# The difference of the two attention maps formed whole by VectorE

## What is computed

```
s = jnp.einsum('bqhmd,bkhmd->bhmqk', qi, k_all).astype(jnp.float32) * scale
p = jax.nn.softmax(s, axis=-1)
a = p[:, :, 0] - lam * p[:, :, 1]
return jnp.einsum('bhqk,bkhe->bqhe', a.astype(v_all.dtype), v_all)
```

## Time and profile before

| what | value |
| --- | --- |
| median of three runs | 2513.55 us |
| profiled execution, first to last instruction | 2509.4 us |
| TensorE busy over the whole span | 2317.3 us, 92% |
| VectorE busy | 1323.7 us, 53% |
| ScalarE busy | 849.3 us, 34% |
| GpSimd busy | 875.1 us, 35% |
| mean granted TensorE clock | 0.974 |

### The profile page before, as it was taken

One profiled execution on the slowest core, in us unless ns is written; L12 is line 12 of the kernel. 1 busy time (PEld: TensorE's weight loads), 2 busy tenths in 40 slices (PEclk: granted clock), 3 DMA queues, 4 the chain that ended last, 5 costly groups with the idle time before them and its releaser, 6 DMA issues. The chain is left out here.

```text
span 2509.4 us, 30851 instructions
## 1 busy us (share of the span) xinstructions
PE 2317.3 (92%) x10898; PEld 1846.8 (74%) x10898; DVE 1323.7 (53%) x1373; ACT 849.3 (34%) x1244; POOL 875.1 (35%) x600
## 2 busy tenths in 40 slices
PE   4799999999968999999999999968888888899998
PEld 2445888888746788887787788857777777788787
DVE  5754339999992200016556540079999995800101
ACT  5745511111101212222222211157777774222221
POOL 0004823333311222221221222136656653844443
PEclk9999999999989999999999999989999997999999
DMA  8977621111111122221221232332221105153433
GB/s 290 337 247 219 193 66 46 50 46 46 46 42 51 55 72 71 67 72 54 72 75 53 72 97 72 87 89 57 59 59 48 48 1 206 67 176 127 160 129 108
DMA packets 227184, 246.46 MB, mean 98 GB/s; under 512 B 11277, under 2 KB 163853, under 8 KB 225583
## 3 DMA queue, kind: packets, MB, share of 16 engines
q1 hardware_dynamic: 225680, 235.11, 29.8%
q0 software_dynamic: 1440, 10.49, 1.1%
HBM read 214.09 MB, written 31.47 MB: 98 GB/s over the span
## 5 line engine op out<-in xcount | busy, mean ns | idle before, releaser
L448 POOL TENSOR_TENSOR w_lo<-w_raw,w_hi 128x512 fp32r<-128x512 f32 x288 | 402.7, 1409 | 1067.3 <-ACT w_hi L700 1066.9
L570 PE MATMUL psum<-h_hi,w_hi 128*128 128x512 f32 x1792 | 561.6, 395 | 6.5 <-POOL w_lo L448 4.9
L570 PE MATMUL psum<-h_hi,w_lo 128*128 128x512 f32 x1792 | 552.8, 390 | 0.0
L570 PE MATMUL psum<-h_lo,w_hi 128*128 128x512 f32 x1792 | 552.6, 390 | 0.0
L700 ACT ACTIVATE w_hi<-w_raw 128x512 fp32r<-128x512 f32 x288 | 180.8, 631 | 1036.9 <-PE psum L570 729.6
L570 PEld LDWEIGHTS psum<-h_hi,w_hi 128*128 128x128 f32 x1792 | 337.3, 188 | 85.3 <-issue 16.5
L570 PEld LDWEIGHTS psum<-h_lo,w_hi 128*128 128x128 f32 x1792 | 337.1, 188 | 70.6
L570 PEld LDWEIGHTS psum<-h_hi,w_lo 128*128 128x128 f32 x1792 | 336.9, 188 | 70.3
L999 DVE SCALAR_TENSOR_TENSOR conv<-y_pad,tap_w,conv 128x1024 f32<-128x1024 f32 x240 | 365.2, 1522 | 9.4
L1675 POOL TENSOR_TENSOR wo_lo<-wo_raw,wo_hi 128x512 fp32r<-128x512 f32 x128 | 175.8, 1380 | 188.4 <-ACT wo_hi L1758 188.4
L84 PE MATMUL psum<-wo_hi,m_hi 128*128 128x512 f32 x512 | 202.0, 395 | 10.7 <-DVE m_lo L1791 6.5
(11 more groups left out here) (174 smaller groups left out, 3182.8 us busy)
## 6 DMA issues: line engine op xcount, KB each, us to landing
w_raw<-in_w_in_dram SPq DMA_DIRECT2D x288, 256.0 KB, 3.0
ada_w<-in_w_ada_dram SPq DMA_DIRECT2D x32, 1024.0 KB, 6.8
wo_raw<-in_w_out_dram SPq DMA_DIRECT2D x128, 256.0 KB, 3.0
proj<-stage SPq DMA_DIRECT2D x40, 512.0 KB, 3.1
gate_w<-in_w_ada_dram SPq DMA_DIRECT2D x16, 1024.0 KB, 5.0
x_tok<-in_x_dram POOLq DMA_DIRECT2D x8, 1024.0 KB, 7.2
k_raw<-proj SPq DMA_DIRECT2D x16, 512.0 KB, 5.7
q_raw<-proj SPq DMA_DIRECT2D x16, 512.0 KB, 6.2
```

Of the source, the lines that this page charges most:

```text
L448: pool.tensor_tensor(w_lo[:, c], w_raw[:, c], w_hi[:, c].bitcast(F32), ALU.subtract).then_inc(w_lo_ready[c], 1)
L570: mm = pe.matmul(bank(2 * s_ + hf), w[:, c, j, :], x[:, jj, hf * BANK:(hf + 1) * BANK], start=(jj == 0 and w is w_hi and x is h_hi), stop= ...
```

## The change

VectorE's scalar_tensor_tensor now covers all 1280 columns. `difference_rest`, its semaphore `rest_ready` and the three places that waited for it (TensorE before round 1 of `turn_diff`, ScalarE before `exp`, GpSimd before its own second instruction and before `low_q`) are gone. GpSimd keeps `low_k` and `low_q` alone, each of which starts as soon as ScalarE's rounding has signalled; between the two kinds stands a wait for GpSimd's own earlier work.

```diff
-    SHARE = 6 * P
...
-                if rd == 1:
-                    pe.wait_ge(rest_ready, 2 * s_ + 2)
...
-                    act.wait_ge(rest_ready, 2 * s_ - 2)
...
-            def difference_rest(st, s_, first=False):
-
-                pool.wait_ge(factor_ready, s_ + 1)
-                if not first:
-                    pool.wait_ge(turned6, use6(s_ - 2, 1) + 1)
-                b = st % 2
-                rest = diff[:, b, SHARE:]
-                pool.tensor_tensor(rest, prob[:, b, 1, SHARE:], map1_factor[:, b:b + 1].to_broadcast([P, KEYS - SHARE]),
-                                   ALU.mult).then_inc(rest_ready, 1)
-                pool.wait_ge(rest_ready, 2 * s_ + 1)
-                pool.tensor_tensor(rest, rest, prob[:, b, 0, SHARE:], ALU.add).then_inc(rest_ready, 1)
-
-            def head(h, b, first=False, last=False):
-                for st in range(TT):
-                    s_ = TT * h + st
-                    if not last or st + 1 < TT:
-                        difference_rest((st + 1) % TT, s_ + 1, first and st == 0)
-                    if not last and st in (1, 2):
-                        low_k(h + 1, 1 - b, st - 1)
-                    if not last and st in (3, 4):
-
-
-                        pool.wait_ge(rest_ready, 2 * s_ + 4)
-                        low_q(h + 1, 1 - b, st - 3)
-                        pool.wait_ge(q_split, 2 * (h + 1) + st - 2)
-
...
+            def head(h, b):
+                for m in range(2):
+                    low_k(h + 1, 1 - b, m)
+                pool.wait_ge(k_split, 2 * (h + 2))
+                for m in range(2):
+                    low_q(h + 1, 1 - b, m)
+                    pool.wait_ge(q_split, 2 * (h + 1) + m + 1)
...
-                nc.vector.scalar_tensor_tensor(out=diff[:, st % 2, 0:SHARE], in0=prob[:, st % 2, 1, 0:SHARE],
-                                               scalar=map1_factor[:, st % 2:st % 2 + 1], in1=prob[:, st % 2, 0, 0:SHARE],
+                nc.vector.scalar_tensor_tensor(out=diff[:, st % 2, :], in0=prob[:, st % 2, 1, :],
+                                               scalar=map1_factor[:, st % 2:st % 2 + 1], in1=prob[:, st % 2, 0, :],
                                                op0=ALU.mult, op1=ALU.add).then_inc(diff_ready, 1)
```

More of the change, by code:

```diff
@@ L1140, in attention @@
     factor_ready = sem("factor_ready")
-    rest_ready = sem("rest_ready")
     diff_ready = sem("diff_ready")
@@ L1377, in low_q @@
                                    ).then_inc(q_split, 1)
-            def difference_rest(st, s_, first=False):
-                pool.wait_ge(factor_ready, s_ + 1)
-                if not first:
-                    pool.wait_ge(turned6, use6(s_ - 2, 1) + 1)
-                b = st % 2
-                rest = diff[:, b, SHARE:]
-                pool.tensor_tensor(rest, prob[:, b, 1, SHARE:], map1_factor[:, b:b + 1].to_broadcast([P, KEYS - SHARE]),
-                                   ALU.mult).then_inc(rest_ready, 1)
-                pool.wait_ge(rest_ready, 2 * s_ + 1)
-                pool.tensor_tensor(rest, rest, prob[:, b, 0, SHARE:], ALU.add).then_inc(rest_ready, 1)
-            def head(h, b, first=False, last=False):
-                for st in range(TT):
-                    s_ = TT * h + st
-                    if not last or st + 1 < TT:
-                        difference_rest((st + 1) % TT, s_ + 1, first and st == 0)
-                    if not last and st in (1, 2):
-                        low_k(h + 1, 1 - b, st - 1)
-                    if not last and st in (3, 4):
-                        pool.wait_ge(rest_ready, 2 * s_ + 4)
-                        low_q(h + 1, 1 - b, st - 3)
-                        pool.wait_ge(q_split, 2 * (h + 1) + st - 2)
-            difference_rest(0, 0, first=True)
-            head(0, 0, first=True)
+            def head(h, b):
[5 more added lines that the diff above has]
+                    pool.wait_ge(q_split, 2 * (h + 1) + m + 1)
+            head(0, 0)
             with pool.Fori(0, HEADS // 2 - 1) as i:
@@ L1410, in _ @@
                 head(2 * i + 2, 0)
-            head(HEADS - 1, 1, last=True)
         @block.vector
```

## The result

The kernel with the whole difference on VectorE takes 2531.46 us in the median (2527.77 to 2534.07, 4 runs), beside 2514.08 for the kernel before in the same session: slower by 17.4 us, ratio 1.0071 [1.0057, 1.0086]. The forecast was 2536.5 in a range of 2519 to 2544, with slower at 0.83. So sign and range hold, the size is 5 us too large. The time is also the very number of rival 1, by coincidence: the trace has the forecast's mechanism, `factor` held, at smaller prices.

What follows compares the result with a forecast made beforehand. VectorE, busy 51.4 of 54 us a head, was taken to set the pace. Per head 1.15 + 1.80 + 0.15 = 3.1 us; seven heads 21.7, last head 1.2: 2513.55 + 22.9 = 2536.5 us, range 2519 to 2544.

Steps and rivals of the forecast that it cites:

- rival 1: Small `factor` is not held by GpSimd, only the difference: 2.4 us a head, 2531.5 us; chance 0.20.
- step 1: Loop step of a head, counted from 0, where the first `k_lo` was to hold `factor`: 1.15 us in all.
- step 3: Loop step of a head, counted from 0, where both `q_st` run and the second holds the difference: 1.80 us.
- `k_lo`, 1.15 forecast: First `k_lo` holds `factor` 1.1 us; with the difference at 1.56 instead of 1.51, 1.15 us a head.
- `q_st`, 1.80 forecast: First `q_st` holds `factor` some 0.7 us, hidden; the second holds the difference, delaying VectorE's next instruction 1.80 us a head.
- The widening: VectorE's difference at 1280 columns takes 1.56 us alone: 0.15 us a head elsewhere, 1.2 us in the last head.
- visible gaps: VectorE's idle times in a head: 0.51 us awaiting an exponential, about 0.5 us awaiting `dT_hi` in each value-turning step.
- Rival 2: GpSimd's splits hold nothing that matters, only the widening costs, some 2.5 to 3.5 us: 2516.5 us; chance 0.11.
- Rival 3: TensorE's wait on GpSimd's product is real, so 9.6 us go: 2507 us; chance 0.06.
- Rival 4: More is held: second `k_lo` catches a `factor`, or 1280 columns take 1.68 us: 2542 to 2550 us; chance 0.11.
- three value steps: Steps of a head that turn values; VectorE's idle wait for `dT_hi` was to hide the 1.56 us difference: cost nothing.

Runs made afterwards that it cites:

- both-placed kernel: Changed kernel with both `k_lo` and both `q_st` on GpSimd waiting for VectorE's differences: 2511.46 us, 0.9988 of the kernel before; longer second series 2512.74 us, 0.9993.
- Q's split placed: Changed kernel with only the two `q_st` waiting for VectorE's differences, `k_lo` as changed: 2519.55 us, 1.0020 of the kernel before.
- 15.3 us less VectorE work: Kernel before (768 columns on VectorE), GpSimd's share started after VectorE's difference, `factor` as one-input `tensor_scalar`: 2515.58 us, 1.0008.
- My three misses: Kernel before, GpSimd's share after VectorE's difference, `tensor_scalar` `factor`; VectorE at 768 columns, 896, or a share by step: 2515.58, 2517.02, 2515.22 us.
- three kernels with such different work on VectorE: Kernel before, and two edits of it with GpSimd's share after VectorE's difference and `tensor_scalar` `factor`: 768 columns (2515.58 us), share by step (2515.22 us).
- the freed VectorE: Kernel before with 768 columns on VectorE, GpSimd's share started after VectorE's difference, `factor` by `tensor_scalar`: 2515.58 us, 1.0008.
- one-input `factor`: Changed kernel with `factor` by `tensor_scalar`, one tile and two per-row scalars, GpSimd's queue as changed: 2532.77 us, 1.0076 of the kernel before.
- Q's split placed and the one-input `factor`: Changed kernel with both `q_st` waiting for VectorE's differences and `factor` by `tensor_scalar`, `k_lo` as changed: 2514.77 us, 1.0007 of the kernel before.

## Why the prediction was right, and where its sizes were off

**The mechanism.** All of its steps are in the trace: least duration of the difference 1.54 (1.56 forecast), one `map_factor` a head in step 1 at 1.20, in the first head 1.48 (about 1.3), one at 0.89 in step 3 (about 0.9), one difference at 2.65 (near 2.5), projections and output as before. The both-placed kernel shows that the two splits are the entire loss: put them behind the difference and the stretch falls by 18.75 us, more than the 17.31 it had gained. The open point, whether a 128 x 1 instruction is held, is settled: yes, and the one-input form beside the same `k_lo` is not. That agrees with the rule cited from the Trainium skill (SBUF — State Buffer, "SBUF: two separate sides"), which names two SBUF inputs and makes no exception for size.

**`k_lo`, 1.15 forecast, 0.98 measured.** `k_lo` starts 1.76 us ahead of `factor` where I placed 1.62: its rounding ends 0.11 earlier in the head, and it starts 0.08 after it, not 0.15. That is 0.14 less hold. The widening that I added behind it isn't seen.

**`q_st`, 1.80 forecast, 1.5 measured.** The hold itself is worth 1.72: step 3 grows by 1.65 with it, by -0.07 with Q's split placed. The pair takes 4.81 us, not 4.92, the gap between them being under a tenth. The other 0.16 is a gain that I had not seen: the wait of `p_inv` goes from 0.51 to 0.32, and step 3's `map_factor` comes 0.15 earlier. The both-placed kernel has the same -0.15 in each steady head, so it belongs to the change without the holds. I did not isolate it.

**The widening, 0.15 a head and 1.2 in the last forecast, 0 and about 0.6 measured.** This is the mis-sized term whose reason matters. I took each 0.05 us on VectorE outside the visible gaps for 0.05 us of the head. In the last head six differences grow by 0.12 each, and only every second one moves the next step, by 0.13; with the 0.28 of the very last (1.54 for the 1.26 of the earlier trace rows) that makes 0.6. In the steady heads nothing is left at all: where nothing is held, in the both-placed kernel, a steady head is 0.24 us shorter than before instead of 0.15 longer.

**The sum.** Forecast 7 x 3.1 + 1.2 = 22.9 us. Measured: the first head 2.65, the second 2.0, five at 2.46, the last 0.3, together 17.3, and 17.4 in the medians. Set against the both-placed kernel a steady head splits up cleanly: the two holds cost 0.97 and 1.72 us, 2.7 together, where 1.1 and 1.80 were forecast, and the rest of the change gives 0.24 back, where it was forecast to cost 0.2. So most of the 0.64 us a head lies in the rest of the change, not in the holds; seven heads multiply it.

**What bounds the kernel, half right.** "A microsecond put on VectorE outside these gaps is a microsecond of the attention" holds for time put where something waits: the 2.7 us of holds in a head came through whole. The opposite, time taken off, does not hold: 15.3 us less VectorE work gave nothing. The 10 us more of the both-placed kernel cost nothing either, but nearly all of that had been forecast to vanish in the gaps. My three misses rest on that reading. That the steady heads of three kernels with such different work on VectorE agree to 0.03 us says that something else sets their length. My reading is another loop, in which VectorE, TensorE and ScalarE wait for each other in turn (transposes, `dT_hi`, `dT_lo`, the product, the next scores, the maximum and the exponential that frees their bank); the waits of VectorE on `dT_hi`, on scores and on the exponential in the trace above are its joints. TensorE alone isn't the pace: with the freed VectorE it still waits 38 of 306 us in the steady heads. That loop is argued from the waits, and which of its links would have to become shorter was not tested and stays open.

**The rivals.** Rival 1 falls by the 1.20 and 0.89 us of `factor`. Rival 2 (no hold, 2516.5) is what the both-placed kernel builds, and even there the widening that it kept costs nothing. Rival 3, TensorE's wait on GpSimd: the purest test is the both-placed kernel, where GpSimd forms no part of the difference and nothing is held. Its waits of TensorE in the steady heads:

```profile
PE psum L1199 <- DVE dT_lo L1453: 21.9, 22, 1.0
PE psum L1199 <- DVE v_lo L1411: 10.2, 16, 0.8
```

Before, these two names had 18.5 and 9.7 us, and GpSimd's 1.7, over the same heads. The transposes wait as long, only by another name: `v_lo` was the true releaser, and the wait that went cost nothing. Rival 4 falls: the second `k_lo` meets no `factor`, and the three value steps hide 1.54 us.

## What to carry to other kernels

Work taken off an engine can cost time through what stood behind it: the splits of K and Q had been timed by GpSimd's part of the difference, and without it they ran into VectorE's instructions with two SBUF tiles as inputs. So when such a part goes, put a wait in its place that keeps GpSimd's long instructions behind these (2531.5 to 2511.5 us here), and count the smallest instruction among those that can be held. And an engine that is busy 95% of a stretch isn't shown to be its pace: take some of its work away, and see whether the stretch gets shorter.

## What the runs showed of the hardware that was not expected

- A 128 x 1 `scalar_tensor_tensor` that begins while GpSimd's `k_lo` runs ends with it: 0.22 us becomes up to 1.48. The same product as `tensor_scalar` with two per-row scalars takes 0.27 us anywhere, 0.05 more than the other form when that one is free.
- A held difference of 1280 columns ends 1.35 us after GpSimd's instruction, whether it began 1.3 us (2.65) or 1.94 us (3.29) ahead of that end; 0.19 us of its 1.54 pass while it is held, as with the 768 columns of the earlier trace rows.
- With the one-input `factor`, TensorE's granted clock fell to 0.5, the level of 1.2 GHz, behind an idle gap of 1.76 to 1.77 us in four heads, and stayed at 1.00 behind the same gap in two. In the kernel after it fell behind a gap of 0.99 to 1.01 us in three heads and stayed in four. So the length of the gap doesn't decide it alone. What a drop costs differs as much: it made the step 1.36 to 1.40 us longer under the products behind the gap, cost 0.5 to 0.7 us in step 3 with Q's split placed and the one-input `factor`, and nothing that could be seen in step 3 of the kernel after, where VectorE is held meanwhile.
